# A four-layer fp32 encoder on one core: new head and a 16-block attention pipeline

## The chip, the cores and the metric

The program runs on one core of a Trainium2 chip. The metric is the device time of one execution in microseconds (us), from three runs. The inputs lie in HBM; weights are streamed to SBUF as they are needed.

## The reference

The input is 512 tokens of 1024 features, float32. Two layers alternate: first windowed attention, then latent attention, each followed by a SwiGLU feed-forward network, and an RMS norm ahead of each. Only the first layer's part is touched:

```python
hn = _rmsnorm(h, norm_mix[0])
qkv = hn @ w_qkv                       # 16 query heads, 4 key and 4 value heads of 64
q, k, v = split(qkv)                   # 1024, 256 and 256 columns
q = q * 64 ** -0.5
scores = einsum('q.k') - slope[head] * |pos_q - pos_k|    # per block of 128 queries,
scores = where(|t - s| <= 128, scores, -1e30)             # keys of the block and its neighbours
p = softmax(concat([scores, sink[head]]))[..., :-1]
h = h + (p @ v) @ w_o
```

With 512 tokens there are four query blocks. The two at the ends see 256 keys, the two in the middle 384.

## The kernel before

**Number format.** TensorE reads fp32r. To keep the accuracy of fp32, each operand is split in two: `hi` is the value rounded to fp32r, `lo` is the rest. A product of two tiles is three matmuls into one PSUM bank: hi by lo, lo by hi, hi by hi (`product`, lines 949, 950, 951). So each weight tile (`w_raw`, one of two slots, 128 partitions by 1024 columns) is loaded, rounded to `w_hi` on GpSimd (`w_split_hi`, line 442) and the rest taken on VectorE (`w_split_lo`, line 1473), before TensorE can use it.

**Engines and order.** There is no scheduler: each engine runs a program written out by hand, and the engines are tied by semaphores. TensorE's order sets the order of the work. A wait stalls everything behind it on its engine.

**Head.** The four tiles of x (128 tokens by 1024) land one after the other. TensorE transposes them (line 1021) into the eight banks, one for each 128 features. ScalarE sums the squares of each tile (line 647), then with VectorE copies the transposed x to `h` (lines 654 and 1542). ScalarE makes `x_hi` from `h` (658), VectorE makes `x_lo` (`x_low`, 1548). Then come the projections, three matmuls for each 128 features: two tiles of keys (48 matmuls of 512 columns), the values (96 of 256), and the first two of eight query tiles (48 of 512). Between the values and the queries VectorE scales the keys into `k_dup` (1584, eight instructions) and builds the distance table `near` (1596, 1599). The second query tile's `w_lo` stands behind all of that.

**Attention.** It runs in four groups, one for each key head, with four query heads each. A unit u of a group is one query block n with one head, 16 in a group. Its steps:

- TensorE: scores of 256 or 384 keys, `product` with the keys in `kp_hi`, `kp_lo`. A head fills 64 of the 128 partitions; keys are padded with zeros, so that each of the three matmuls has 128 rows. Three banks are used in turn.
- VectorE: adds the distance and takes the maximum (`read_scores`, 1658), ScalarE: exponential and sum (`expo`, 712), VectorE: reciprocal (1643), GpSimd: scales the row (509).
- TensorE: transposes the four heads' probabilities, 128 keys at a time (1088), ScalarE and VectorE: their hi and lo (718, 1666).
- TensorE: values (`values`, two products for each 128 keys), ScalarE and VectorE: `ot_hi` (722) and `ot_lo` (1671).

At the end of a group the next group's queries (`a_q_out`, 1621; `a_q_lo`, 1627), keys (1606) and values (1613) are made ready. The remaining six query tiles, and in the last group parts of the output projection `w_o`, are put between these steps. The scores of block n+1 come before the transposes of block n, and the values of block n-1 behind them.

**Output projection.** `wo_phase` follows; the profile's TensorE reaches its loop's second tile at 184 us. Everything from there on is not touched.

## Time and profile before

| | us |
|---|---|
| median of 3 runs | 1250.78 (1250.13 to 1253.23) |
| the profiled execution | 1250.18 |
| its span | 1248.4 |
| TensorE busy in the span | 1191.3 (95%) |
| VectorE busy | 630.4 (50%) |
| first product of the head, start | 14.73 |
| first scores, start | 55.48 |
| output projection's loop, start | 184.16 |

The span is the time from the first to the last instruction. TensorE's busy time is modelled: each matmul shows a duration longer than the distance to the next one's start, since they are pipelined. What a matmul costs in a dense stretch is therefore read from the distance between neighbours' starts. The share of busy time is a mean over stages; what the change is worth is read from the stages up to 184 us.

### The profile page before, as it was taken

What the parts mean: (1) busy time and instruction counts of PE and PEld (TensorE: products, weight loads), DVE (VectorE), ACT (ScalarE), POOL (GpSimd) and SP (SyncE); (2) the same over time, 40 slices, a digit from 0 to 9 for tenths busy, and PEclk for the clock granted to TensorE, in tenths of its full rate; (3) what the DMA queues carried; (4) which work ended last, traced back from release to release, by engine and by line L of the source; (5) the groups of instructions that cost most, each with busy time, mean ns of one, the idle gap of its engine ahead of it and who ended that gap; (6) DMA issues with size and microseconds to landing.
All of it is one profiled execution on the core that took longest, in us unless ns stands there. A gap on an engine that the chain in (4) does not pass through costs nothing.

```text
span 1248.4 us, 18246 instructions
## 1 busy us (share of the span) xinstructions
PE 1191.3 (95%) x5796; PEld 992.8 (80%) x5796; DVE 630.4 (50%) x1067; ACT 354.0 (28%) x689; POOL 399.0 (32%) x415
## 2 busy tenths in 40 slices
PE   6899999999999999999889999899999999999996
PEld 5788878788888888888867777678788888888885
DVE  6777764433333433454576776744443333343432
ACT  4266652222200111111365665632222200111101
POOL 3343335333311333343241412325233311323342
PEclk8999999999999999999989999999999999999998
DMA  6211113232433233333200101013333332333421
GB/s 161 68 34 35 35 34 101 85 99 86 119 93 89 87 101 101 109 93 91 70 20 18 36 0 34 18 39 114 97 89 101 103 115 68 101 96 89 120 81 67
DMA packets 176475, 96.67 MB, mean 77 GB/s; under 512 B 8752, under 2 KB 173104, under 8 KB 176432
## 3 DMA queue, kind: packets, MB, share of 16 engines
q1 hardware_dynamic: 176432, 96.12, 26.5%
q8 instruction: 24, 0.39, 0.1%
q14 instruction: 19, 0.16, 0.0%
HBM read 94.01 MB, written 2.10 MB: 77 GB/s over the span
## 4 chain that ended last, share of the span: by engine, by line
PE 80%; DVE 9%; issue 4%; ACT 3%; POOL 2%; DMA 1%; ACTq 0%; DVEq 0%; POOLq 0%; SPq 0%
PE bank L949 26%; PE bank L951 25%; PE bank L950 25%; PE bank L1391 2%; DVE w_lo L1473 1%; POOL w_hi L442 1%; DVE stat L2004 1%; DVE apt_lo L1666 1%; PE bank L1088 1%; DVE s_a L1658 1%; DVE bpt_lo L2009 1%; DMA x_n<-in_x 1%; ACT s_b L880 1%; ACT bpt_hi L886 0%; DVE w_lo L1490 0%
## 5 line engine op out<-in xcount | busy, mean ns | idle before, releaser
L1473 DVE TENSOR_TENSOR w_lo<-w_raw,w_hi 128x1024 fp32r<-128x1024 f32 (+2 forms) x151 | 203.2, 1346 | 297.8 <-POOL w_hi L442 297.7
L442 POOL TENSOR_SCALAR w_hi<-w_raw 128x1024 fp32r<-128x1024 f32 (+3 forms) x159 | 183.3, 1153 | 421.4 <-PE bank L951 410.0
L949 PE MATMUL bank<-x_hi,w_lo 128*128 128x512 f32 x784 | 308.3, 393 | 9.9 <-DVE w_lo L1473 7.7
L951 PE MATMUL bank<-x_hi,w_hi 128*128 128x512 f32 x784 | 306.3, 391 | 0.0
L950 PE MATMUL bank<-x_lo,w_hi 128*128 128x512 f32 x784 | 306.3, 391 | 0.0
L949 PEld LDWEIGHTS bank<-x_hi,w_lo 128*128 128x128 f32 x784 | 147.8, 189 | 42.1 <-DVE w_lo L1473 5.5
L951 PEld LDWEIGHTS bank<-x_hi,w_hi 128*128 128x128 f32 x784 | 147.7, 188 | 30.9
L950 PEld LDWEIGHTS bank<-x_lo,w_hi 128*128 128x128 f32 x784 | 148.0, 189 | 29.7
L949 PE MATMUL bank<-f_hi,w_lo 128*128 128x512 f32 x352 | 137.8, 391 | 1.0 <-DVE f_lo L1776 1.0
L951 PE MATMUL bank<-f_hi,w_hi 128*128 128x512 f32 x352 | 137.1, 389 | 0.0
L950 PE MATMUL bank<-f_lo,w_hi 128*128 128x512 f32 x352 | 137.0, 389 | 0.0
L546 POOL TENSOR_TENSOR gate_s<-gate_s,rs_t 128x512 f32<-128x512 f32 x44 | 56.7, 1290 | 141.7 <-ACT gate_s L769 141.7
L607 POOL TENSOR_SCALAR s_b<-s_b,stat 128x512 f32<-128x512 f32 x64 | 47.3, 741 | 131.5 <-DVE stat L1643 131.3
L1738 DVE TENSOR_TENSOR h<-h,bank 128x512 f32 (+1 forms) x40 | 27.5, 687 | 115.4 <-PE bank L951 115.4
L772 ACT ACTIVATE f_hi<-hid 128x512 f32 x44 | 27.8, 632 | 202.2 <-DVE hid L1774 202.2
L949 PEld LDWEIGHTS bank<-f_hi,w_lo 128*128 128x128 f32 x352 | 66.1, 188 | 15.4 <-DVE f_lo L1776 1.9
L951 PEld LDWEIGHTS bank<-f_hi,w_hi 128*128 128x128 f32 x352 | 66.1, 188 | 13.7
L950 PEld LDWEIGHTS bank<-f_lo,w_hi 128*128 128x128 f32 x352 | 66.1, 188 | 13.5
L769 ACT ACTIVATE gate_s<-gate_t 128x512 f32<-128x512 f32 x44 | 27.8, 632 | 160.5 <-DVE gate_t L1763 160.2
L456 POOL TENSOR_TENSOR ss<-ss,sq 128x512 f32<-128x512 f32 x28 | 52.3, 1870 | 39.6 <-ACT sq L636 39.5
L2009 DVE TENSOR_TENSOR bpt_lo<-bank,bpt_hi 128x512 fp32r<-128x512 f32 x64 | 43.8, 685 | 35.3 <-ACT bpt_hi L886 35.2
L949 PE MATMUL bank<-ot_hi,w_lo 128*128 128x512 f32 x128 | 50.4, 394 | 3.3 <-DVE w_lo L1473 2.6
(219 smaller groups left out, 1863.6 us busy)
## 6 DMA issues: line engine op xcount, KB each, us to landing
w_raw<-in_ffn_w_gu SPq DMA_DIRECT2D x88, 512.0 KB, 3.8
w_raw<-in_ffn_w_down SPq DMA_DIRECT2D x32, 704.0 KB, 4.4
w_raw<-in_a_w_qkv SPq DMA_DIRECT2D x12, 512.0 KB, 3.8
w_raw<-in_a_w_o SPq DMA_DIRECT2D x8, 512.0 KB, 3.6
w_raw<-in_b_w_o SPq DMA_DIRECT2D x8, 512.0 KB, 3.8
w_raw<-in_b_w_in SPq DMA_DIRECT2D x4, 672.0 KB, 4.0
w_raw<-in_b_w_uq SPq DMA_DIRECT2D x4, 576.0 KB, 4.0
x_n<-in_x SPq DMA_DIRECT2D x4, 512.0 KB, 5.3
```

The lines of the kernel that those rows point to most:

```text
L442: pool.tensor_scalar(split_part(w_hi, s, cols, kv), raw_part(s, cols, kv), 1.0, 1.0, ALU.mult, ALU.mult) \
L456: pool.tensor_tensor(n.ss[:], n.ss[:], n.sq[:, b, :], ALU.add).then_inc(ss_ready, 1)
L546: pool.tensor_tensor(gate_s[:], gate_s[:], rs_t[:], ALU.mult).then_inc(silu_rs_ready, 1)
L607: pool.tensor_scalar(view, view, stat[:, 2, u % 8:u % 8 + 1], 1.0, ALU.mult, ALU.mult) \
L769: act.activation(gate_s[:], gate_t[:], ACT.Silu).then_inc(silu_ready, 1)
L772: act.activation(f_hi[:, j, :], hid[:], ACT.Copy).then_inc(f_hi_ready, 1)
L949: pe.matmul(o, ll, rh, start=start, stop=False)
L950: pe.matmul(o, lh, rl, start=False, stop=False)
L951: return pe.matmul(o, lh, rh, start=False, stop=stop)
L1473: dve.tensor_tensor(split_part(w_lo, s, cols, kv), raw_part(s, cols, kv), f(split_part(w_hi, s, cols, kv)), ALU.subtract) \
L1738: dve.tensor_tensor(dst, h[:, m, :], banks[6 + bank_s][:], ALU.add).then_inc(proj_free, 1)
L2009: dve.tensor_tensor(bpt_lo[:, n % 2, i, :], banks[3 + i % 2][:], f(bpt_hi[:, n % 2, i, :]), ALU.subtract).then_inc(pt_free, 1)
```

## The change

It rewrites the program up to the output projection, on all engines.

- **Head.** x_hi and x_lo are made straight from the transposed x in PSUM, and ScalarE alone copies it to `h` afterwards. The key weights are split in halves. The squares of the last x tile are taken later. Eight small matmuls of the identity run ahead of the first product. The features' order is 6, 7, 4, 5, 0, 1, 2, 3. The first two query tiles have buffers of their own (`q_raw0`, `q_raw1`), are loaded right behind the key weights, rounded on ScalarE, and projected right behind the keys; the values come last.
- **Keys.** No zero padding. `ks` holds two key heads in the halves of the 128 partitions, `kx` the same with the halves swapped; four DMAs from SBUF to SBUF write `kx`. All four heads' keys and values are split once, ahead of the attention.
- **Scores.** Each matmul has 64 rows: the upper or the lower half of the array. Those of two heads alternate (partitions 0 to 63, 64 to 127), into two banks.
- **Pipeline.** 16 blocks (a group's query block with its four heads) run in one pipeline over the groups. In slot b TensorE does the scores of block b, the transposes of block b-1 and the values of block b-2, with query or w_o products between them.
- **Weights in the attention.** From the fifth query tile on, `w_hi` is made on ScalarE (`a_w_hi`) and `w_lo` on GpSimd (`a_w_lo`). Reciprocals are taken for two heads at once.

The core of the diff (of the head, the scores and the weights; the slots' order stands in the excerpts below it):

```diff
-            for pos, m in enumerate(K_ORDER):
-                if pos % 2 == 0:
-                    act.wait_ge(pt_done, pos + 2)
-                    act.activation(h[:, K_ORDER[pos + 1], :], banks[K_ORDER[pos + 1]][:], ACT.Copy).then_inc(h_act, 1)
...
-                act.activation(x_hi[:, m, :], h[:, m, :], ACT.Copy, scale=gains[:, 0, m, :]).then_inc(x_hi_ready, 1)
+            def x_high(pos):
+                act.wait_ge(pt_done, pos + 1)
+                act.activation(x_hi[:, K_ORDER[pos], :], banks[K_ORDER[pos]][:], ACT.Copy,
+                               scale=gains[:, 0, K_ORDER[pos], :]).then_inc(x_hi_ready, 1)
...
+            pe.wait_ge(h_act, 1)
+            pe.wait_ge(x_ready, 1)
+            for i in range(8):
+                pe.matmul(banks[6][:, 0:P], ident[:], ident[:], start=True, stop=True)
+            for s in range(2):
+                for pos in range(KD // 2):
+                    k_block(pos, s)
+            for s in range(2):
+                for pos in range(KD // 2, KD):
+                    k_block(pos, s)
+            pe.wait_ge(h_act, 3)
+            spread(norms[0])
...
+            sp.wait_ge(ks_ready, 2)
+            for src, dst in ((ks_hi, kx_hi), (ks_lo, kx_lo)):
+                for half in range(2):
+                    there, here = slice((1 - half) * HD, (2 - half) * HD), slice(half * HD, (half + 1) * HD)
+                    sp.dma_start(f(dst[there, :, :]), f(src[here, :, :])).then_inc(kx_in, 16)
...
-                def scores(u):
-                    n, hd = u // HG, u % HG
-                    k0, nk = A_KB[n]
-                    before = 16 * g + (u - 2 if u >= 3 else (0, -2, -1)[u])
-                    pe.wait_ge(s_free, S_A + before)
-                    q = (slice(None), hd // 2, slice(n * P, (n + 1) * P))
-                    k = (slice(None), hd % 2, slice(k0 * P, (k0 + nk) * P))
-                    product(banks[u % 3][:, 0:nk * P], aq_hi[q], aq_lo[q], kp_hi[k], kp_lo[k], True, True) \
-                        .then_inc(s_done, 1)
+            def a_scores(b, i):
...
+                    pe.wait_ge(a_read, 4 * (b - 1) + 2 * i + 2)
...
+                for k_low, q_low in ((False, True), (True, False), (False, False)):
+                    for odd in range(2):
+                        rows = slice(odd * HD, (odd + 1) * HD)
+                        q = (aq_lo if q_low else aq_hi)[rows, g % 2, i, n * P:(n + 1) * P]
+                        here = odd == g % 2
+                        kt = (ks_lo if here else kx_lo) if k_low else (ks_hi if here else kx_hi)
+                        ins = pe.matmul(banks[A_SCORE_BANKS[2 * i + odd]][:, 0:nk * P], q,
+                                        kt[rows, g // 2, k0 * P:(k0 + nk) * P],
+                                        start=q_low, stop=not (k_low or q_low))
...
+            def a_w_hi(c2, s):
+                act.wait_ge(w_in[s], 16 * c2 + 16)
+                act.wait_ge(w_used, 2 * c2 + s - 1)
+                act.wait_ge(w_hi_ready, 2 * c2 + s)
+                act.activation(w_hi[s][:, 0:W_COLS], w_raw[s][:, 0:W_COLS], ACT.Copy).then_inc(w_hi_ready, 1)
...
+            def a_w_lo(c2, s):
+                pool.wait_ge(w_hi_ready, 2 * c2 + s + 1)
+                pool.wait_ge(w_ready, 2 * c2 + s)
+                pool.tensor_tensor(w_lo[s][:, 0:W_COLS], w_raw[s][:, 0:W_COLS], f(w_hi[s][:, 0:W_COLS]), ALU.subtract)
...
+            for b in range(1, A_BLOCKS + 2):
...
+                elif n == 2:
+                    scores(0)
+                    scores(1)
+                    fill(1)
+                    turn(0)
+                    turn(1)
+                    fill(2)
+                    values(0)
+                    values(1)
+                    turn(2)
```

VectorE's order in the head before, from the first copies of the transposed x (`h` from a bank) on:

```order
L1542 COPY h_49<-bank6 128x512 [waits pt_done]
L1542 COPY h_49<-bank0 128x512 [waits pt_done]
L1548 SCALAR_TENSOR_TENSOR x_lo_51<-h_49,gains_65,x_hi_50 128x512 [waits x_hi_ready,gain_in]
L1473 TENSOR_TENSOR w_lo0_58<-w_raw0_54,w_hi0_56 128x1024 [waits w_hi_ready]
L1548 SCALAR_TENSOR_TENSOR x_lo_51<-h_49,gains_65,x_hi_50 128x512 [waits x_hi_ready]
L1473 TENSOR_TENSOR w_lo1_59<-w_raw1_55,w_hi1_57 128x1024 [waits w_hi_ready]
L1516 TENSOR_SCALAR ms_n_64<-sums_n_72 128x8 [waits x_sq_ready]
L1519 RECIPROCAL rs_n_63<-ms_n_64 128x8 [waits rms_n]
```

The same place now, up to the last key half:

```order
L1740 SCALAR_TENSOR_TENSOR x_lo_51<-bank6,gains_65,x_hi_50 128x512 [waits x_hi_ready,gain_in]
L1747 TENSOR_TENSOR w_lo0_58<-w_raw0_54,w_hi0_56 128x512 [waits k_hi_half]
L1740 SCALAR_TENSOR_TENSOR x_lo_51<-bank7,gains_65,x_hi_50 128x512 [waits x_hi_ready]
L1740 SCALAR_TENSOR_TENSOR x_lo_51<-bank4,gains_65,x_hi_50 128x512 [waits x_hi_ready]
L1740 SCALAR_TENSOR_TENSOR x_lo_51<-bank5,gains_65,x_hi_50 128x512 [waits x_hi_ready]
L1747 TENSOR_TENSOR w_lo1_59<-w_raw1_55,w_hi1_57 128x512 [waits k_hi_half]
L1740 SCALAR_TENSOR_TENSOR x_lo_51<-bank0,gains_65,x_hi_50 128x512 [waits x_hi_ready]
L1747 TENSOR_TENSOR w_lo0_58<-w_raw0_54,w_hi0_56 128x512 [waits k_hi_half]
L1740 SCALAR_TENSOR_TENSOR x_lo_51<-bank1,gains_65,x_hi_50 128x512 [waits x_hi_ready]
L1740 SCALAR_TENSOR_TENSOR x_lo_51<-bank2,gains_65,x_hi_50 128x512 [waits x_hi_ready]
L1747 TENSOR_TENSOR w_lo1_59<-w_raw1_55,w_hi1_57 128x512 [waits k_hi_half]
```

The copies are gone, `x_lo` reads the bank, the key weights' rests come in halves of 512 columns, and the norm's small steps have moved behind them.

TensorE at the start of a group's scores before (group 1; `kp` keys, `aq` queries, all of 128 rows, one head after the other):

```order
L949 MATMUL bank0<-kp_hi_83,aq_lo_81 128x256 [waits s_free,q_ready,kp_ready]
L950 MATMUL bank0<-kp_lo_84,aq_hi_80 128x256
L951 MATMUL bank0<-kp_hi_83,aq_hi_80 128x256
L949 MATMUL bank1<-kp_hi_83,aq_lo_81 128x256 [waits s_free]
L950 MATMUL bank1<-kp_lo_84,aq_hi_80 128x256
L951 MATMUL bank1<-kp_hi_83,aq_hi_80 128x256
L949 MATMUL bank6<-x_hi_50,w_lo0_58 128x512 [waits proj_free,w_ready]
```

And now (group 1, second pair of heads; in this group the even head takes its keys from `kx`, the odd one from `ks`):

```order
L1224 MATMUL bank2<-kx_hi_84,aq_lo_81 128x256 [waits q_ready,a_read]
L1224 MATMUL bank7<-ks_hi_82,aq_lo_81 128x256
L1224 MATMUL bank2<-kx_lo_85,aq_hi_80 128x256
L1224 MATMUL bank7<-ks_lo_83,aq_hi_80 128x256
L1224 MATMUL bank2<-kx_hi_84,aq_hi_80 128x256
L1224 MATMUL bank7<-ks_hi_82,aq_hi_80 128x256
L1083 MATMUL bank6<-x_hi_50,w_lo0_58 128x512
```

There are as many matmuls as before, with the same columns; they alternate between two banks and between the halves of the array.

## Rows read from the trace of the kernel before

**Rows 1.** The page: span, and busy us of each engine.

```profile
span 1248.4 us, 18246 instructions
...
PE 1191.3 (95%) x5796; PEld 992.8 (80%) x5796; DVE 630.4 (50%) x1067; ACT 354.0 (28%) x689; POOL 399.0 (32%) x415
```

**Rows 2.** Windows: busy us of each engine (x instructions), granted clock, DMA.

```profile
14.60:21.40 6.80, 5.91 (x13) 4.26 (x14) 6.42 (x13) 4.24 (x9) 0.78 (x1) 0.50 0.81 143
...
47.20:49.90 2.70, 0.00 (x0) 0.00 (x0) 2.64 (x4) 1.26 (x2) 2.70 (x4) 1.00 0.00 0
...
55.50:182.70 127.20, 122.40 (x785) 108.97 (x783) 93.39 (x280) 76.74 (x203) 43.88 (x78) 1.00 0.12 34
```

**Rows 3.** Waits of TensorE up to 183 us: total us, times, longest.

```profile
PE bank L949 <- DVE w_lo L1473: 7.7, 3, 4.2
```

**Rows 4.** Timeline of TensorE, 4 to 22 us: start, us, instruction, idle before.

```profile
9.44 1.09 PE L1021 MATMUL bank<-ident,x_n 128*128 128x128 f32 x8 [0.41 <-DMA x_n<-in_x]
14.73 0.77 PE L949 MATMUL bank<-x_hi,w_lo 128*128 128x512 f32 x1 [4.20 <-DVE w_lo L1473]
...
18.55 0.63 PE L949 MATMUL bank<-x_hi,w_lo 128*128 128x512 f32 x1
18.98 0.63 PE L950 MATMUL bank<-x_lo,w_hi 128*128 128x512 f32 x1
...
21.71 0.40 PE L951 MATMUL bank<-x_hi,w_hi 128*128 128x512 f32 x1
21.95 0.39 PE L949 MATMUL bank<-x_hi,w_lo 128*128 128x512 f32 x1
```

**Rows 5.** Timeline of TensorE in the attention: starts of neighbours.

```profile
55.59 0.28 PE L950 MATMUL bank<-kp_lo,aq_hi 128*128 128x256 f32 x1
55.71 0.28 PE L951 MATMUL bank<-kp_hi,aq_hi 128*128 128x256 f32 x1
...
59.94 0.34 PE L950 MATMUL bank<-kp_lo,aq_hi 128*128 128x384 f32 x1
60.12 0.33 PE L951 MATMUL bank<-kp_hi,aq_hi 128*128 128x384 f32 x1
...
77.58 0.60 PE L1088 MATMUL bank<-ident,s_a 128*128 128x128 f32 x4
77.93 0.48 PE L949 MATMUL bank<-x_hi,w_lo 128*128 128x512 f32 x1
78.25 0.39 PE L950 MATMUL bank<-x_lo,w_hi 128*128 128x512 f32 x1
```

**Rows 6.** Groups by shape, TensorE, 55.4 to 182.7 us: busy, mean ns, idle.

```profile
L949 PE MATMUL bank<-kp_hi,aq_lo 128*128 128x384 f32 x32 | 11.3, 353 | 0.7 <-DVE stat L1658 0.7
...
L949 PE MATMUL bank<-kp_hi,aq_lo 128*128 128x256 f32 x32 | 10.0, 311 | 0.3
```

**Rows 7.** Groups by shape, VectorE, then ScalarE, 55 to 183 us.

```profile
L1666 DVE TENSOR_TENSOR apt_lo<-bank,apt_hi 128x512 fp32r<-128x512 f32 x40 | 27.3, 685 | 5.8 <-ACT apt_hi L718 5.4
L1658 DVE CUSTOM_DVE_ANT_0 s_a<-near,bank,minus_sink 128x384 f32<-128x384 f32 x32 | 19.2, 599 | 0.9 <-PE bank L951 0.8
...
L712 ACT ACTIVATE s_a<-s_a,stat 128x385 f32<-128x385 f32 x32 | 19.6, 615 | 7.0 <-DVE stat L1658 6.8
```

**Rows 8.** Timeline of VectorE, then GpSimd, in the head.

```profile
11.78 1.56 DVE L1548 SCALAR_TENSOR_TENSOR x_lo<-h,gains,x_hi 128x512 fp32r<-128x512 f32 x1 [0.61 <-ACT x_hi L658]
13.26 1.21 DVE L1473 TENSOR_TENSOR w_lo<-w_raw,w_hi 128x1024 fp32r<-128x1024 f32 x1
...
18.73 1.40 DVE L1548 SCALAR_TENSOR_TENSOR x_lo<-h,gains,x_hi 128x512 fp32r<-128x512 f32 x2
...
11.76 1.04 POOL L442 TENSOR_SCALAR w_hi<-w_raw 128x1024 fp32r<-128x1024 f32 x1 [10.24 <-DMA w_raw<-in_a_w_qkv]
13.84 1.54 POOL L442 TENSOR_SCALAR w_hi<-w_raw 128x1024 fp32r<-128x1024 f32 x1 [1.04 <-DMA w_raw<-in_a_w_qkv]
```

**Rows 9.** The page: a tensor-by-tensor addition on GpSimd.

```profile
L456 POOL TENSOR_TENSOR ss<-ss,sq 128x512 f32<-128x512 f32 x28 | 52.3, 1870 | 39.6 <-ACT sq L636 39.5
```

More of the change, by code:

```diff
@@ L64 @@
 W_UKV = KVL // P * HG * 2 * HD
-U_K, U_Q, U_WOA = 0, 2, 10
+U_K, U_WOA = 0, 2
 U_FFN0 = U_WOA + KD
@@ new lines, in _ @@
+            pe.wait_ge(h_act, 3)
+            spread(norms[0])
+            pe.wait_ge(vec_consts, 1)
+            pe.wait_ge(h_act, 5)
+            for i in range(2):
+                pe.wait_ge(q01_ready, i + 1)
+                for k in range(KD):
+                    at = slice(k * P, (k + 1) * P)
+                    last = product(banks[3 + i][:], q01_hi[i][:, at], q01_lo[i][:, at], x_hi[:, k, :], x_lo[:, k, :],
+                                   k == 0, k == KD - 1)
+                last.then_inc(q01_used, 1)
@@ new lines, in a_v @@
+            def a_v(t):
+                if t == 0:
+                    pe.wait_ge(proj_free, 1)
+                if t == 1:
+                    pe.wait_ge(o_free, O_NORM0 + 1)
+                if t >= 2:
+                    pe.wait_ge(v_ready, t - 1)
+                cols = GROUPS * HD
+                for k in range(KD):
+                    if t == 0 and k % 4 == 0:
+                        pe.wait_ge(w_ready, C_V + k // 4 + 1)
+                    wh, wl = w_block(k // 4, cols, k % 4)
+                    at = slice(t * P, (t + 1) * P)
+                    last = product(banks[6 - t % 2][:, t // 2 * cols:(t // 2 + 1) * cols], x_hi[:, k, at], x_lo[:, k, at],
+                                   wh, wl, k == 0, k == KD - 1)
+                if t < NT - 1:
+                    last.then_inc(v_done, 1)
+                else:
+                    last.then_inc(w_used, 2)
@@ new lines, in a_turn @@
+            def a_turn(b, i):
+                unit = a_unit(b, i)
+                if b == 0 and i < 2:
+                    pe.wait_ge(q_tmp_ready, i + 1)
+                else:
+                    pe.wait_ge(pt_free, unit - 1)
+                for j, hd in enumerate((0, 2, 1, 3)):
+                    if i == 0 and j != 2:
+                        pe.wait_ge(p_ready, 4 * b + hd + 1)
+                    last = pe.transpose(banks[3 + unit % 2][:, j * P:(j + 1) * P],
+                                        s_a[:, b % 2, hd, 1 + i * P:1 + (i + 1) * P], ident[:])
+                last.then_inc(pt_done, 1)
@@ new lines, in a_values @@
+            def a_values(b, i):
+                k0, nk = a_keys(b)
+                pe.wait_ge(pt_free, a_unit(b, i) + 1)
+                if i == 0:
+                    pe.wait_ge(o_free, O_A + b)
+                    if b == 0:
+                        pe.wait_ge(av_zero, 2)
+                        pe.wait_ge(v_ready, NT)
+                for odd in range(2):
+                    at = (2 * (b // NT) + 1 - odd) * HD
+                    v = (slice(None), k0 + i, slice(at, at + P))
+                    p = (slice(None), b % 2, i, slice(2 * P * odd, 2 * P * (odd + 1)))
+                    last = product(banks[5][:, 0:2 * P], av_hi[v], av_lo[v], apt_hi[p], apt_lo[p],
+                                   i == 0 and odd == 0, i == nk - 1 and odd == 1)
+                if i == nk - 1:
+                    last.then_inc(o_done, 1)
@@ new lines, in a_q_step @@
+            def a_q_step(m, k):
+                c = C_Q + m - 2
+                if k == 0:
+                    pe.wait_ge(w_ready, c + 1)
+                    if m == 2:
+                        pe.wait_ge(v_ready, 3)
+                    else:
+                        pe.wait_ge(q_tmp_ready, m)
+                wh, wl = w_block(m % 2, P, k)
+                last = product(banks[6][:], wh, wl, x_hi[:, k, :], x_lo[:, k, :], k == 0, k == KD - 1)
+                if k == KD - 1:
+                    last.then_inc(w_used, 1)
@@ L1547, in x_low, with k_low @@
                 dve.wait_ge(x_hi_ready, pos + 1)
-                dve.scalar_tensor_tensor(x_lo[:, m, :], h[:, m, :], gains[:, 0, m, :], f(x_hi[:, m, :]),
+                dve.scalar_tensor_tensor(x_lo[:, m, :], banks[m][:], gains[:, 0, m, :], f(x_hi[:, m, :]),
                                          ALU.mult, ALU.subtract).then_inc(x_ready, 1)
-            read_x(0)
-            read_x(2)
+            def k_low(s, part):
+                dve.wait_ge(k_hi_half, 2 * s + part + 1)
+                half = K_HALVES[part]
+                dve.tensor_tensor(w_lo[s][:, half], w_raw[s][:, half], f(w_hi[s][:, half]), ALU.subtract) \
+                    .then_inc(w_ready if part else k_lo_half, 1)
```

891 lines of the change are left out of this document (492 added, 399 removed).

## The prediction

> **What bounds the kernel now.** I read the page first: TensorE is busy 95% of the span, and the next engine, VectorE, 50% [rows 1]. So only two things can shorten the run: a stretch where TensorE stands still, and fewer TensorE cycles. The change ends at the output projection, so the second view was TensorE by windows up to 183 us [rows 2], then its waits there [rows 3], then its timeline in the head and the attention [rows 4, 5], then the groups by shape [rows 6, 7] and the other engines in the head [rows 8]. The reader is to see in them: a head in which TensorE first waits and then runs at the lower of its two clock levels (granted clock 0.50, which is 1.2 GHz); a hole of 2.7 us before the second query tile; an attention of 127.2 us that is nearly full of matmuls.
>
> **Prices.** At the full clock neighbours start 0.23 to 0.24 us apart for 512 columns [rows 4], 0.12 for 256 and 0.17 to 0.18 for 384 [rows 5]. I use 0.23, 0.12 and 0.175. Four transposes take 0.35 us (0.09 each), and the matmul behind them holds its successor off for 0.32 instead of 0.23, so leaving the transposes costs 0.09 [rows 5]. At the lower clock 512 columns take 0.43 [rows 4].
>
> **The attention before, as a sum.** 55.5 to 182.7 us is 127.2 us [rows 2]. In it stand 144 query and 48 w_o matmuls of 512 columns (192 x 0.23 = 44.2), 240 of the values (28.8), 192 of the scores, half of each shape [rows 6] (three lines, of which one stands there, with 32 of either shape; 96 x 0.12 + 96 x 0.175 = 28.3), and 160 transposes with 28 exits (14.0 + 2.5). Sum 117.8, so TensorE stands still for about 9.4 us there.
>
> **The change, part by part.**
>
> *Head up to the keys.* Before, the last transposes start at 9.44 and the first product at 14.73, with 4.20 us of waiting for `w_lo` [rows 4]. VectorE's chain in it is x_lo of 1.56 at 11.78, w_lo of 1.21 at 13.26 [rows 8]. Now the copies to h are gone and the first `w_lo` is half as wide (0.6). GpSimd starts its rounding at 11.76, when the weights land [rows 8]; half of its 1.04 puts the first half at 12.3, VectorE adds 0.6 and about 0.4 of hand-over: 13.3. The eight identity matmuls need x_lo and the copy of one bank (about 12.1) and take 8 x 0.11, so they end at 13.0 and are hidden. First product 13.4: gain 1.3. The wait of 0.75 between first and second product (the 7.7 us in three waits are 4.20, 0.75 and 2.72 [rows 3]) goes, since the first tile alone is now used four times: 0.75. The supply: seven more x_lo at 0.70 (1.40 for two) and three half w_lo at 0.6 end at about 20.2 [rows 8]; TensorE needs the last x_lo at 13.4 + 39 x 0.23 = 22.4 at the earliest. So the 48 key matmuls run without a hole.
>
> *The clock.* The granted clock was 0.50 from 14.6 to 21.4 [rows 2], right behind the stretch of 4.2 us in which TensorE had nothing to do. About 16 matmuls started at 0.43 instead of 0.23: 3.2 us. Now the idle stretch is 10.4 to 12.1, and the identity matmuls follow. I take it that the clock stays up: 3.2. Bounds: 3.2 and 0. The Trainium skill, "TensorE: Matmul & The Clock Gate", Part 4, says that transposes don't count as busy for the clock; by that rule the clock would be low at the first product whatever stands between, and the 3.2 us would be lost. The rows speak against it: the page grants 1.00 until 14.6 with nothing but transposes ahead.
>
> *Behind the keys.* The second query tile's hole of 2.72 us [rows 3], a window without one matmul while VectorE is busy 2.64 of 2.70 [rows 2], goes: both query tiles now stand ahead of the values, and the keys' scaling (2 instructions instead of 8), the table and the values' `w_lo` run beside 11.0 us of query matmuls (48 x 0.23). VectorE has some 10 us of work there, so it is just covered; the values might wait up to 1 us. The first query scale needs the query's end, a rounding on ScalarE and a rest on VectorE (three steps of 0.7) before the second pair of block 0's scores: 0.5 us late. New holes in the head: 1.0. Behind the values, query tile 3's weights can be split only when the values' have been used, GpSimd 1.04 and VectorE 1.2, of which scores and transposes of block 1 cover 1.5: 0.8, counted below. The four DMAs to `kx` start when the keys' rests are there (about 30) and have 9 us until the first scores; none of the kind is in the trace, the tiles of 512 KB take 3.8 us from issue to landing. Head in sum: 1.3 + 0.75 + 3.2 + 2.7 - 1.0 = 7.0.
>
> *Scores in halves.* No matmul of 64 rows is in the trace. Bounds for a pair: both at the price of one, 0.12 or 0.175; or one after the other, 0.24 or 0.35. Each still loads its own stationary operand of 128 columns; a transpose shows a load and a matmul every 0.09 [rows 5], so two loads take up to 0.175. I take 0.175 for both shapes: 96 x 0.175 = 16.8, against 28.3: gain 11.5. Bounds 14.2 in all (gain 14.1) and 28.3 (gain 0). The Trainium skill, "TensorEngine Tiling (Array Packing)", Tiling Modes, Key Properties, says that tiles run in parallel but that a change of the mode drains the engine. No row here shows either. There are 38 such changes (19 runs of score matmuls). I price each like the exit from the transposes, 0.09: 3.4 lost. Bounds 0 and 0.16 each (the modelled 0.28 of a matmul less its 0.12 [rows 5]), 6.1.
>
> *The pipeline.* Transposes come a slot behind the scores and values a slot behind them. The four waits of transposes for `apt_lo` and one of the values lay in these 9.4 us. VectorE had 93.4 us of work in 127.2 [rows 2]; six of eight `w_lo`, the padded keys and half of the reciprocals leave it. One slot costs TensorE about 6.6 us, VectorE 4 to 6 (apt_lo 0.69, maximum 0.60 [rows 7]), ScalarE up to 6.3 in the slots with a `w_hi` (four exponentials of 0.62 [rows 7], three roundings of 0.6, one of the weights at 1.0, and two small ones). None is over TensorE, but one is near it. GpSimd's addition of 512 columns takes 1.87 [rows 9], so `a_w_lo` of 1024 takes up to 3.7; behind it stand the next block's scalings, which are needed a slot later, so I cost it at nothing; without that cover it would be 3.7 six times. Of the 9.4 us of stalls I leave 4.5 (0.8 of it the one above, 0.5 at the last values): gain 4.9. Bounds: 2 left, or 12.
>
> Sum: 7.0 + 11.5 - 3.4 + 4.9 = 20.0 us. The profiled execution's 1250.2 gives 1230.2; it lies 0.6 below the median, so the run's median would be 1230.8, and I say 1231.
>
> **Rivals.**
>
> *The halves don't overlap.* The pair takes the time of both: 11.5 less, 1242. For it: each matmul has its own load, and the loads already fill 109 of 127 us [rows 2]. Against it: different rows, different banks, alternating.
>
> *The chain of a block becomes the bound.* Maximum, exponential, reciprocal, scaling, transpose, rounding, rest now all wait for each other over a slot of 6.6 us, where a block took 127.2 / 16 = 7.9. If VectorE's waits for ScalarE (ScalarE at 6.3 in one slot of four, `w_hi` ahead of the exponentials) cost 0.75 a slot, 16 slots give 12: 1243. For it: VectorE is idle for 5.4 us behind ScalarE's `apt_hi` already [rows 7]. Against it: the work between covers most of it.
>
> *The head gives nothing.* Clock low as before and `kx` or the values' weights some us late: 7.0 lost, 1238. For it: SP issues the kx transfers behind everything else.
>
> *Slower.* Each 64-row matmul waits for its load and lets the array run empty: then it costs its modelled duration, 0.31 and 0.35 [rows 6], and 192 of them 63.7 us instead of 16.8: 47 lost, 1278. It decides from 36.8 us of scores on, 0.19 us a matmul. For it: the mode changes. Against it: the order of the loads is the same as now, where they run ahead.
>
> **Chances.** Forecast 0.50; no overlap 0.18; chain 0.14; head 0.08; slower 0.07; that the parts cancel to no change 0.03. The forecast's own range is 1224 to 1237 (overlap at 14.2 and free mode changes below; all mode changes at 0.16 and a low clock above). With the rivals on the fast side, 1222 to 1246 holds 8 in 10. A difference under 0.3% (3.8 us) can't be told from none in this kernel. Faster 0.90, same 0.03, slower 0.07.
>
> **What the profile after would show.** Granted clock 1.00 from the first product on, which starts at 13 to 14 us; keys' matmuls 0.23 apart; scores of block 0 at about 39; block 1 at about 49; pairs of score matmuls that start within a few ns or with 0.175 for two; the output projection's second tile at 164 instead of 184.2. VectorE's waits for ScalarE grow if the chain rules; pairs at 0.24 and 0.35 mean no overlap. The prediction is wrong if the projection starts before 158 or after 176, or if the time behind it changes by more than 3.5 us, the price of one more or one less stretch at the lower clock.

## The result, and the profile after

The changed kernel takes 1235.26 us (median of 4 runs, 1233.6 to 1236.35), the kernel before 1251.18 us beside it. The ratio is 0.987, with a 95% interval of 0.9853 to 0.9887: 16 us faster. Forecast were 1231 us and a range of 1222 to 1246. The profiled execution took 1235.2 us, its span is 1233.1 us.

The page after, span and busy us of each engine (against [rows 1]):

```profile
span 1233.1 us, 18213 instructions
...
PE 1181.3 (96%) x5812; PEld 980.3 (79%) x5812; DVE 609.2 (49%) x1013; ACT 355.8 (29%) x692; POOL 406.4 (33%) x423
```

TensorE is busy 10.0 us less, VectorE 21.2 less, GpSimd 7.4 more. Windows of the changed kernel (busy us and count of each engine, granted clock, DMA), the keys' products and then block 1's scores to the last output projection step that the attention holds (against [rows 2]):

```profile
14.60:21.40 6.80, 6.80 (x31) 5.63 (x31) 5.39 (x9) 6.78 (x11) 0.00 (x0) 1.00 0.79 208
50.10:165.90 115.80, 111.94 (x773) 94.22 (x772) 77.47 (x222) 70.72 (x190) 51.91 (x82) 1.00 0.13 37
```

The keys' products now run at granted clock 1.00 where it was 0.50. The attention is 115.8 us long, without block 0's scores, which stand ahead of it and take 0.9; together 116.7 where it was 127.2. VectorE has 77.5 us of work in it instead of 93.4. Waits of TensorE up to 185 us (total, times, longest; against [rows 3]):

```profile
PE bank L1083 <- DVE w_lo L1669: 2.8, 2, 1.5
PE bank L1164 <- ACT h L736: 1.6, 1, 1.6
PE bank L1240 <- DVE apt_lo L1848: 1.1, 2, 0.9
PE bank L1224 <- DVE aq_lo L1816: 0.7, 1, 0.7
```

The three waits of 7.7 us are gone. In the first line stand a new one of 1.53 us, for query tile 2's weights behind the values, and one of 1.31 at the output projection that both kernels have.

TensorE at the head's turn from transposes to products (start, us, instruction, idle before; against [rows 4]):

```profile
12.08 2.05 PE L1164 MATMUL bank<-ident 128*128 128x128 f32 x16 [1.58 <-ACT h L736]
13.88 0.48 PE L1083 MATMUL bank<-x_hi,w_lo 128*128 128x512 f32 x1
```

The first product starts at 13.88 instead of 14.73. And the first two score pairs of block 2 with their neighbours (against [rows 5]):

```profile
59.39 0.39 PE L1085 MATMUL bank<-x_hi,w_hi 128*128 128x512 f32 x1
59.71 0.44 PE L1224 MATMUL bank<-ks_hi,aq_lo 64*128 64x384 f32 x1
59.71 0.44 PE L1224 MATMUL bank<-kx_hi,aq_lo 64*128 64x384 f32 x1
59.99 0.33 PE L1224 MATMUL bank<-ks_lo,aq_hi 64*128 64x384 f32 x1
...
60.16 0.34 PE L1224 MATMUL bank<-ks_hi,aq_hi 64*128 64x384 f32 x1
...
60.70 0.34 PE L1224 MATMUL bank<-kx_hi,aq_hi 64*128 64x384 f32 x1
60.96 0.50 PE L1083 MATMUL bank<-x_hi,w_lo 128*128 128x512 f32 x1
61.30 0.39 PE L1084 MATMUL bank<-x_lo,w_hi 128*128 128x512 f32 x1
```

Both matmuls of a pair start together (59.71 and 59.71). The next pairs follow 0.175 apart, so a pair costs what one matmul cost in [rows 5]. Around them stand four small losses: 0.32 instead of 0.23 from the last full matmul to the first pair, 0.28 instead of 0.175 behind the first pair, 0.26 instead of 0.175 on leaving, and 0.34 instead of 0.23 behind the first full matmul: 0.4 us a visit. The groups that answer to [rows 7], and the new ones of the weights, 50 to 166 us:

```profile
L1848 DVE TENSOR_TENSOR apt_lo<-bank,apt_hi 128x512 fp32r<-128x512 f32 x40 | 26.9, 685 | 11.4 <-ACT apt_hi L811 11.0
...
L802 ACT ACTIVATE s_a<-s_a,stat 128x385 f32<-128x385 f32 x32 | 19.4, 608 | 5.6 <-DVE stat L1834 5.4
...
L548 POOL TENSOR_TENSOR w_lo<-w_raw,w_hi 128x1024 fp32r<-128x1024 f32 x6 | 14.4, 2406 | 0.0
...
L818 ACT ACTIVATE w_hi<-w_raw 128x1024 fp32r<-128x1024 f32 x6 | 6.3, 1045 | 0.0
```

VectorE waits longer for ScalarE's `apt_hi` than before (11.0 against 5.4) and has time for it. GpSimd's `w_lo` takes 2.4 us, not up to 3.7, and the matmuls that read it don't appear among the waits.

The mark that the prediction calls the output projection's second tile was forecast at 164 and is at 167.39. Where the 16.8 us up to it (from 184.16) come from, against the forecast of 20.0:

| part | forecast | measured |
|---|---|---|
| head, to block 1, without block 0's scores | 7.0 | 6.3 |
| scores' pairs | 11.5 | 14.1 |
| changes of the array's rows | -3.4 | -6.3 to -7.2 |
| stalls in the attention, 9.4 before: gain | 4.9 (4.5 left) | 2.7 to 3.6 (5.8 to 6.7 left) |
| untouched part behind | 0 | -1.5 |

The head is 55.5 less 50.14, plus the 0.9 of block 0's scores. The scores' 14.1 is the count of matmuls at the spacing above. The changes are 18 visits at the 0.35 to 0.40 us that e5 and e2 below give: the prediction counted 19, but the second scores of block 12 and the first of block 13 stand next to each other (135.13 and 135.59 us), which makes one visit of two. The stalls are what 116.7 us leave when the sum of the steps (117.8 less 14.1) and the changes are taken off. Of them 4.5 us can be named: 1.7 for the weights behind the values, and 2.8 in four places of the last group, from 136.7 to 153.9 us, where transposes wait for `apt_lo` and for a scaling and scores for a maximum. Behind the projection's start the span has 1065.7 us instead of 1064.2. Of the total, 16.8 less 1.5 is the 15.3 between the spans.

### The profile page after: what moved, and what is told of

Read it like the earlier page. It is cut to its first block, busy times and chain, and to the rows that moved or that the text cites. A ratio compares the mean times of both kernels' runs of the same rounds, so it can differ in the third digit from the quotient of the medians.

```text
span 1233.1 us, 18213 instructions
## 1 busy us (share of the span) xinstructions
PE 1181.3 (96%) x5812; PEld 980.3 (79%) x5812; DVE 609.2 (49%) x1013; ACT 355.8 (29%) x692; POOL 406.4 (33%) x423
## 4 chain that ended last, share of the span: by engine, by line
PE 84%; DVE 6%; issue 4%; ACT 3%; POOL 2%; DMA 0%; ACTq 0%; DVEq 0%; POOLq 0%
PE bank L1083 26%; PE bank L1085 26%; PE bank L1084 25%; PE bank L1587 2%; PE bank L1240 1%; PE bank L1224 1%; POOL w_hi L482 1%; DVE stat L2215 1%; DVE w_lo L1669 1%; DVE bpt_lo L2220 1%; ACT s_b L1014 1%; PE bank L1158 0%; DVE w_lo L1686 0%; ACT bpt_hi L1020 0%; ACT s_a L802 0%
## 5 line engine op out<-in xcount | busy, mean ns | idle before, releaser
L1669 DVE TENSOR_TENSOR w_lo<-w_raw,w_hi 128x1024 fp32r<-128x1024 f32 (+2 forms) x142 | 191.4, 1349 | 289.1 <-POOL w_hi L482 289.1
L482 POOL TENSOR_SCALAR w_hi<-w_raw 128x1024 fp32r<-128x1024 f32 (+3 forms) x150 | 174.2, 1162 | 404.9 <-PE bank L1085 404.8
L1083 PE MATMUL bank<-x_hi,w_lo 128*128 128x512 f32 x768 | 301.7, 393 | 3.8 <-DVE gate_t L1974 2.2
L1085 PE MATMUL bank<-x_hi,w_hi 128*128 128x512 f32 x768 | 299.1, 389 | 0.0
L1084 PE MATMUL bank<-x_lo,w_hi 128*128 128x512 f32 x768 | 299.0, 389 | 0.0
L1083 PEld LDWEIGHTS bank<-x_hi,w_lo 128*128 128x128 f32 x768 | 144.2, 188 | 35.1 <-DVE gate_t L1974 2.6
L1085 PEld LDWEIGHTS bank<-x_hi,w_hi 128*128 128x128 f32 x768 | 144.2, 188 | 30.5
L1084 PEld LDWEIGHTS bank<-x_lo,w_hi 128*128 128x128 f32 x768 | 144.2, 188 | 29.0
L1084 PEld LDWEIGHTS bank<-f_lo,w_hi 128*128 128x128 f32 x352 | 66.1, 188 | 13.5
L2220 DVE TENSOR_TENSOR bpt_lo<-bank,bpt_hi 128x512 fp32r<-128x512 f32 x64 | 43.8, 686 | 35.3 <-ACT bpt_hi L1020 35.2
L556 POOL TENSOR_SCALAR s_a<-s_a,stat 128x256 f32<-128x256 f32 (+1 forms) x64 | 33.5, 538 | 61.2 <-DVE stat L1843 60.9
```

The source lines that it names most:

```text
L482: pool.tensor_scalar(split_part(w_hi, s, cols, kv), raw_part(s, cols, kv), 1.0, 1.0, ALU.mult, ALU.mult) \
L556: pool.tensor_scalar(view, view, stat[:, 2, u % 8:u % 8 + 1], 1.0, ALU.mult, ALU.mult).then_inc(p_ready, 1)
L1083: pe.matmul(o, ll, rh, start=start, stop=False)
L1084: pe.matmul(o, lh, rl, start=False, stop=False)
L1085: return pe.matmul(o, lh, rh, start=False, stop=stop)
L1669: dve.tensor_tensor(split_part(w_lo, s, cols, kv), raw_part(s, cols, kv), f(split_part(w_hi, s, cols, kv)), ALU.subtract) \
```

## Experiments

For the attention I compare one distance, from block 1's first score to the last values: 111.7 us in the changed kernel (50.14 to 161.83). It is free of what happens in the head and behind. The granted clock is 1.00 all through it in every trace but that of e4.

**Order of a pair.**

```
for k_low, q_low in (...):          ->   for odd in range(2):
    for odd in range(2):                     for k_low, q_low in (...):
```

> The changed kernel, with the six 64-row matmuls of a pair of heads in another order: the three of one head first (rows 0 to 63), then the three of the other (rows 64 to 127), instead of alternating. Nothing else differs. Theory A (two tiles of 64 rows run side by side only when neighbours in the queue lie in different rows): the pairs of one start are gone except where the first head's last meets the second head's first; five steps of 0.12 or 0.175 us instead of three for six matmuls, so 32 x 2 x 0.15 = 9.4 us more than the changed kernel's 1235.3: 1244 to 1246, and the output projection's second tile near 177 instead of 167.4. Rival B (the array keeps separate queues of rows and overlaps whatever stands in the other half): no loss, 1235. Rival C (each 64-row matmul costs its load when the rows repeat): 0.3 us a matmul, 192 x 0.3 = 58 against 14: 1279.

Measured: 1234.52 us, ratio 0.986 (0.9837 to 0.9884), distance 111.7. Rival B holds. TensorE in this kernel, with three matmuls of one head queued ahead of three of the other:

```profile
95.12 0.38 PE L1224 MATMUL bank<-kx_hi,aq_lo 64*128 64x256 f32 x1
95.13 0.38 PE L1224 MATMUL bank<-ks_hi,aq_lo 64*128 64x256 f32 x1
95.34 0.28 PE L1224 MATMUL bank<-kx_lo,aq_hi 64*128 64x256 f32 x1
95.35 0.28 PE L1224 MATMUL bank<-ks_lo,aq_hi 64*128 64x256 f32 x1
```

The other head's `aq_lo` matmul, three places behind in the queue, starts 0.01 us after the first. Alternating is not what gives the overlap.

**Same rows, and all rows.**

```
rows = slice(odd * HD, (odd + 1) * HD)   ->   slice(0, HD)      (e7)
                                         ->   slice(0, P)       (e5)
```

> The changed kernel with the score matmuls of both heads on rows 0 to 63 (the second head then gets the first one's numbers, so its result is not the one wanted; count, columns, banks and order are unchanged). Theory A (the matmuls of e1 overlapped since they lay in different rows, whatever their order): here nothing overlaps, each of 192 takes 0.12 or 0.175 us, 14.1 us more with the visits' cost kept: 1249.5, the first values to the last 14 us longer. Rival B (two 64-row matmuls into different banks overlap whatever their rows): 1235.4. Rival C (in the same rows each waits for its own load to be over): 0.3 us each, 43 us more, 1279.

Measured: 1246.53 us, ratio 0.9952 (0.994 to 0.9965), distance 122.6, 10.9 more. The matmuls follow each other at 0.175 and nothing overlaps:

```profile
93.64 0.33 PE L1224 MATMUL bank<-ks_lo,aq_hi 64*128 64x384 f32 x1
93.81 0.33 PE L1224 MATMUL bank<-kx_hi,aq_hi 64*128 64x384 f32 x1
93.99 0.34 PE L1224 MATMUL bank<-ks_hi,aq_hi 64*128 64x384 f32 x1
```

That is Theory A. The blocks 1 to 15 hold 13.4 of the 14.1 us of doubled steps (7 blocks x 6 x 0.12 and 8 x 6 x 0.175). TensorE's idle steps (starts more than 0.25 us later than the prices of the prediction have them) fall from 4.5 to 1.7 us, as each slot is longer: 13.4 - 2.8 = 10.6, and 10.9 is what came.

> The changed kernel with every score matmul on all 128 rows (the same tiles, both heads' rows at once, so the scores are sums over two heads and not the ones wanted; count, columns and banks are unchanged). It has neither the overlap of two 64-row matmuls nor the change of the array's rows. Theory A (the changed kernel saves 14.1 us by the overlap and pays 19 x 0.4 = 7.6 us for the visits): 6.5 us more, block 1 to the last values 118.2 instead of 111.7 us, 1242.5. Rival B (the prediction's 3.4 us for the changes): 10.7 us more, 1247. Rival C (the 0.4 of a visit is no matter of the rows and stays): 14.1 more, 1250.

Measured: 1240.64 us, ratio 0.9917 (0.9896 to 0.9938), distance 116.9, 5.2 more. On 128 rows a visit has no edges: the first score matmul starts 0.23 behind the last one of 512 columns, and the others follow at 0.12:

```profile
96.66 0.28 PE L1224 MATMUL bank<-kx_hi,aq_lo 128*128 128x256 f32 x1
96.78 0.28 PE L1224 MATMUL bank<-ks_hi,aq_lo 128*128 128x256 f32 x1
96.90 0.28 PE L1224 MATMUL bank<-kx_lo,aq_hi 128*128 128x256 f32 x1
```

Doubled steps 13.4, less 2.1 of idle steps that go, less the price of the 17 visits in this distance, is 5.2: a visit costs 0.36 us. Theory A had 0.4 and was 1.3 too high in sum; the prediction's 0.18 (Rival B) is out by more.

**More visits.**

```
scores(0)                 scores(0)
scores(1)         ->      fill(1)
turn(0)                   scores(1)
fill(2)                   turn(0); fill(1)
```

> The changed kernel, with one step of 128-row matmuls (a query or output projection step of three 512-column matmuls) moved between the first and the second pair of heads in 11 of the 15 blocks 1 to 15, those with block number mod 4 of 1, 2, 3 (block 1 excepted). No matmul is added; only the number of times at which TensorE goes from full rows to 64 rows and back rises, from 19 to 30. Theory A (a visit costs what the trace of the changed kernel suggests, about 0.4 us): 11 x 0.4 = 4.4 us more, 1239.7. Rival B (the prediction's price, 2 x 0.09 a visit): 2.0 us more, 1237.3. Rival C (changes are free and the 0.4 has another reason, such as the wait for a bank): within 0.5 us, 1235.3.

Measured: 1238.75 us, ratio 0.9902 (0.9879 to 0.9924), distance 116.1: 4.4 more for 11 visits, of which 0.5 are idle steps. So 0.35 to 0.40 a visit, with e5's 0.36 between. A visit of three pairs, between a full matmul at either side:

```profile
96.09 0.40 PE L1085 MATMUL bank<-x_hi,w_hi 128*128 128x512 f32 x1
96.42 0.38 PE L1224 MATMUL bank<-kx_hi,aq_lo 64*128 64x256 f32 x1
...
96.64 0.28 PE L1224 MATMUL bank<-kx_lo,aq_hi 64*128 64x256 f32 x1
...
96.77 0.28 PE L1224 MATMUL bank<-ks_hi,aq_hi 64*128 64x256 f32 x1
96.97 0.50 PE L1083 MATMUL bank<-x_hi,w_lo 128*128 128x512 f32 x1
97.31 0.40 PE L1084 MATMUL bank<-x_lo,w_hi 128*128 128x512 f32 x1
```

0.33, 0.22, 0.20 and 0.34 stand where 0.23, 0.12, 0.12 and 0.23 would without edges. Theory A holds.

**The eight identity matmuls.**

```
-            for i in range(8):
-                pe.matmul(banks[6][:, 0:P], ident[:], ident[:], start=True, stop=True)
```

> The changed kernel without the eight matmuls of identity by identity in front of the first product of the keys. Theory A (they hold the clock up after the wait of 1.6 us): a stretch at granted clock 0.50 of some 7 us begins near 14 us, 16 matmuls take 0.43 instead of 0.23 us, 3.2 us more: 1238.5. Rival B (the wait in front of the keys' first product, 10.5 to 13.9 us, is now too short to make the clock fall, and the identity matmuls do nothing): the clock stays at 1.00 and the time is 1235.3, at most 0.3 lower. Where the clock falls in the head it may also fall at another place later, so up to 1.5 us either way can come from the latent attention.

Measured: 1234.18 us, ratio 0.9864 (0.9841 to 0.9887). The first product starts at 12.58 and all behind it at the full clock:

```profile
12.58 0.47 PE L1083 MATMUL bank<-x_hi,w_lo 128*128 128x512 f32 x1 [2.73 <-DVE w_lo L1745]
12.89 0.39 PE L1084 MATMUL bank<-x_lo,w_hi 128*128 128x512 f32 x1
```

By this run Rival B holds, and I took the identity matmuls for useless. e8 and e10 below correct that. The trace shows one of four executions, and a quick one: the weights landed early in it (GpSimd's first rounding starts at 10.63, in e10 at 11.72). Two of the others took 1235.38 and 1236.34 us at a mean granted clock of 0.991 and 0.989, where the profiled one has 0.993; whether the clock fell in their heads isn't known.

**The weights' division put back.**

```
-                        a_w_hi(C_Q // 2 + g + 1, 0)                 (ScalarE)
-                        a_w_lo(C_Q // 2 + g + 1, 0)                 (GpSimd)
+                        w_split_hi(C_Q // 2 + g + 1, 0, W_COLS)     (GpSimd)
+                        w_split_lo(C_Q // 2 + g + 1, 0, W_COLS)     (VectorE)
```

> The changed kernel with the division of the six query and output weights of blocks 2 to 14 put back as in the kernel before: the rounding w_hi on GpSimd (where its subtraction stood), the rest w_lo on VectorE at the end of the same slot; ScalarE has neither. Theory A (the weights were hidden either way; VectorE has 4 to 6 us of work in a slot of 6.6 us): within 1 us of 1235.3. Rival B (VectorE's chain sets the pace of a slot): six times 1.2 us more on VectorE, of which most reaches TensorE, 5 to 7 us: 1241. Rival C (ScalarE was the late one, its rounding of 1.0 us in front of the roundings of the transposes): up to 2 us faster, 1233.5.

Measured: 1245.32 us, ratio 0.9947 (0.9926 to 0.9967), distance 121.2, 9.5 more. None of the three theories was large enough. The waits, 50 to 176 us, then a wait late in the attention and a window behind it:

```profile
DVE w_lo L1666 <- POOL w_hi L482: 8.8, 8, 2.2
...
PE bank L1080 <- DVE ot_lo L1851: 5.7, 4, 2.3
...
147.73 0.35 PE L1080 MATMUL bank<-apt_hi,av_lo 128*128 128x256 f32 x1 [2.34 <-DVE ot_lo L1851]
...
148.88:152.29 3.41, 3.41 (x21) 3.05 (x19) 2.31 (x8) 2.53 (x7) 2.43 (x5) 0.50 0.30 90
```

VectorE now stands still for 8.8 us in front of `w_lo` (e12 below: 1.7), and TensorE waits 5.7 us for `ot_lo`, which VectorE owes it behind that. GpSimd's rounding comes late: it stands behind scalings that wait for VectorE's reciprocals. One part of the 9.5 us is the clock: behind the wait of 2.34 us it stood at 0.50 from 148.88 to 152.29 us, and set against the changed kernel, matmul by matmul, TensorE fell back there from 7.7 to 9.2 us, by 1.6.

> Half of e4: ScalarE keeps the rounding w_hi at the head of the slot, as in the changed kernel, and only the rest w_lo is taken back to VectorE, where e4 had it (behind the last reciprocal of block 4g, behind the last apt_lo of block 4g+2); GpSimd has neither. From block 1's scores to the last values the changed kernel takes 111.7 us and e4 121.2. Theory A (VectorE, with 1.2 us more in six slots, is what made e4 slow): 119 to 121 us, and the time is near 1243. Rival B (e4's loss came from GpSimd's rounding, which stood behind scalings that wait for the reciprocals and so came too late, and VectorE stood still behind it): 112 to 113.5 us, the time near 1236.

Measured: 1239.85 us, ratio 0.9905 (0.9875 to 0.9935), distance 114.9, 3.2 more. Neither theory alone: of e4's 9.5 us 3.2 are VectorE's added work and 1.6 the fallen clock; the other 4.7 came with the rounding that was late on GpSimd and held VectorE up. This holds for the places I chose in the slots; other places were not tried.

**Query tile 2's weights in halves.**

```
 pool: w_hi[0] in two halves;  dve: w_lo[0] half by half
 dve:  w_lo[1] behind a_pt_lo(0, 1) of block 1, instead of ahead of its maxima
 pe:   a_q_step(2, 0) waits for the first half, a_q_step(2, 4) for the second
```

> The changed kernel with the split of query tile 2's weights done in two halves (GpSimd rounds columns 0 to 511, VectorE takes their rest while GpSimd does the others), and query tile 3's rest on VectorE moved behind the work of block 1. Theory A (TensorE's wait of 1.53 us at 53.6 us is the whole chain of one rounding of 1.0 and one rest of 1.6 us, and only the first half is needed): the wait falls to 0.1 to 0.4, 1.2 us less up to the output projection (second tile's start 166.2 instead of 167.4). Rival B (the first transposes of block 1 or its maximum are next and take the gain): under 0.4 us. In the time either may be masked by up to 1.5 us in the latent attention, according to where the clock falls there: 1232.5 to 1235.5.

Measured: 1233.59 us, ratio 0.986 (0.9839 to 0.9881), distance 111.2, 0.5 less. The two places on TensorE:

```profile
52.42 0.50 PE L1088 MATMUL bank<-x_hi,w_lo 128*128 128x512 f32 x1
...
60.81 0.47 PE L1088 MATMUL bank<-x_hi,w_lo 128*128 128x512 f32 x1 [0.91 <-DVE q_tmp L1819]
```

The wait at the first product of query tile 2 is gone, but the first product of tile 3 now waits 0.91 us for the scaling of tile 2, since the moved `w_lo` stands ahead of it on VectorE. Rival B, though with another name in it than I had.

**Combinations.**

```
e8:  e6; no identity matmuls; a_v(0), a_v(1), scores of block 0, a_v(2), a_v(3)
e9:  e6; the same order of the values; w_lo[1] between block 1's two reciprocals;
     the output projection's third tile with its weights in halves too
e10: e9 without the identity matmuls
```

> The halved weights, the identity matmuls left out, and block 0's scores behind the second tile of the values instead of the first (with that tile's two steps on ScalarE and VectorE in front of block 0's exponentials and maxima), so that the second query tile's rest is ready in time. Theory A (each takes away a wait that ended last): 1.2 for the weights, 1.3 for the identity matmuls, 0.7 to 1.3 for the query's rest: the output projection 3.2 to 3.8 us earlier than in the changed kernel, and with the cold stretch in the latent attention at its cheap place another 1.5: 1230.5 to 1232. Rival B (block 0's later chain makes block 1's transposes wait): 1 to 2 us of it lost, 1233.

Measured: 1234.44 us, ratio 0.9867 (0.9846 to 0.9889). No faster than e6, and slower than either theory had it. In its head TensorE waited 3.0 us for `w_lo`, and eight matmuls behind it started 0.43 us apart, 1.6 us in all. Neither theory had that.

> The changed kernel with the identity matmuls kept and four waits attacked: query tile 2's weights in halves; tile 3's rest moved on VectorE between block 1's two reciprocals; block 0's scores behind the second tile of the values; the third output projection tile's weights in halves too. Theory A (the waits of 1.53, 0.69 and 1.31 us go or shrink to 0.4 and nothing takes their place): the output projection's third tile starts 2.5 to 3.2 us earlier than 167.4, at 164.2 to 164.9, and the time is 1232 with the costly place of the cold stretch in the latent attention, 1230.5 with the cheap one. Rival B (as in e6, a third to a half of it comes back as a wait for the next thing VectorE owes): 1.2 us, 1234.

Measured: 1231.3 us (5 runs, 1230.49 to 1232.91), ratio 0.984 (0.9823 to 0.9856), the fastest kernel of the study. The changed kernel, run again beside it (e11), took 1233.03 us: 1.7 more by the medians, 3.3 by the ratios (0.0026 x 1251), with intervals that overlap. So the times alone don't settle the gain; the trace does, for the part that was changed. At the mark of 167.39 it shows

```profile
164.78 0.50 PE L1096 MATMUL bank<-ot_hi,w_lo 128*128 128x512 f32 x1 [0.61 <-DVE w_lo L1998]
```

2.6 us earlier, though its first product came 0.48 us later (14.36): 3.1 us gained in between, as Theory A had it. The wait is 0.61 instead of 1.31.

> The kernel e9 without the eight identity matmuls. Theory A (they matter in the executions in which the weights land late: with a wait of 2.7 us in e3 the clock stayed up, with one of 3.0 in e8 eight matmuls behind it started at 0.43 us): where the wait in front of the first product is 2.7 or less, the time equals e9's or is up to 0.5 lower; where it is 3.0 or more, the granted clock falls behind it for 3.5 us and it costs 1.5 to 2 us. Rival B (e8's cold stretch had nothing to do with them): a cold stretch in the head shows up in e9 as often as here.

Measured: 1233.01 us, ratio 0.985 (0.9825 to 0.9875). The window behind the first product without the identity matmuls:

```profile
14.60:18.00 3.40, 3.40 (x10) 2.58 (x9) 3.40 (x7) 3.40 (x6) 0.13 (x1) 0.52 0.77 180
```

and with them (e9):

```profile
14.60:18.00 3.40, 3.40 (x16) 2.78 (x16) 3.40 (x7) 3.40 (x6) 0.06 (x1) 1.00 0.68 158
```

TensorE without them, at the first product and where the clock has fallen:

```profile
13.67 0.47 PE L1096 MATMUL bank<-x_hi,w_lo 128*128 128x512 f32 x1 [2.90 <-DVE w_lo L1777]
...
15.02 0.63 PE L1098 MATMUL bank<-x_hi,w_hi 128*128 128x512 f32 x1
15.44 0.63 PE L1096 MATMUL bank<-x_hi,w_lo 128*128 128x512 f32 x1
```

The wait was 2.90 us here and the clock fell 1 us behind it, 3.0 us in e8 with the same, 2.73 us in e3 and it stayed up. All ten traces with the identity matmuls show 1.00 in this stretch. The length of the wait doesn't decide alone: in e4's attention the clock fell 1.15 us behind a wait of only 2.34 us, with TensorE busy 5.55 of the 8.88 us before. The identity matmuls hold the first product back (in the changed kernel the half `w_lo` ends at 12.3 and the product starts at 13.88, in e3 it starts at 12.58, of which 0.7 us are left at block 1: 49.46 against 50.14), and are worth some 1.5 (eight starts at 0.43 instead of 0.23) in the executions in which the weights land late. At the mark e10 is 0.9 us behind e9 (165.70 and 164.78). Three traces without them are few; what made the clock stay up in e3 and fall in e8 and e10 stays open.

**The changed kernel again.**

> The changed kernel itself once more, for the untouched part behind it. From the start of the latent projections to the first values of the latent attention the traces show 42.2 to 42.6 us in before, e2, e3, e4, e5, e6 and 43.8 in the changed kernel, e1 and e7; the granted clock falls 21 to 23 us behind the start in the ones and 26.5 in the others. Theory A (which of the two comes is a matter of the execution, not of the kernel): this trace may show either, and over executions the time scatters by 1.5 us; seeing 42.3 here settles it. Rival B (the change or what lies where in memory fixes it): 43.8 again.

Measured: 1233.03 us (1232.72 to 1237.12), ratio 0.9866 (0.9842 to 0.9889). From the first transposes of the latents to the first values of the latent attention, in the changed kernel's first trace:

```profile
593.98 0.38 PE L1472 MATMUL bank<-ident,lat 128*128 128x128 f32 x2
...
637.76 0.48 PE L1083 MATMUL bank<-bpt_hi,bv_lo 128*128 128x512 f32 x1
```

and in its second one:

```profile
593.70 0.38 PE L1472 MATMUL bank<-ident,lat 128*128 128x128 f32 x2
...
635.88 0.48 PE L1083 MATMUL bank<-bpt_hi,bv_lo 128*128 128x512 f32 x1
```

43.8 and 42.2 us, with the same instructions. The windows at the lower clock, of the first and of the second:

```profile
620.40:627.50 7.10, 6.91 (x25) 6.01 (x25) 3.36 (x9) 4.08 (x13) 4.11 (x6) 0.52 0.01 3
```

```profile
615.37:622.20 6.83, 6.71 (x17) 4.74 (x16) 5.17 (x12) 3.88 (x9) 2.07 (x3) 0.50 0.00 1
```

In the first the clock falls 26.4 us behind those transposes and TensorE then has 25 matmuls to do at half speed; in the second it falls 21.7 us behind them, at 615.37, and there are 17. Over all traces: with one stretch that begins 20 to 23 us behind the transposes, 42.2 to 42.6 us (before, e2, e3, e4, e5, e6, e11); beginning at 26.4 to 26.7 (the changed kernel, e10), or with a second one behind it (e1, e7, e9), 43.8 to 43.9 (e12, with a second one too, 43.1); with a stretch of only some 3 us (e8), 41.2. Theory A holds: the 1.5 us lost behind the change is a matter of the execution. The times show it too: of the nine executions of the kernel before that ran beside e11, the five at a mean granted clock of 0.989 to 0.991 took 1249.0 to 1250.9 us, the four at 0.987 1252.4 to 1252.9.

## Why the prediction was right, point by point

*Head up to the keys, 1.3 and 0.75.* First product at 13.88 where I had 13.4, so 0.85 instead of 1.3. VectorE was earlier than I had it, at about 12.3, since the weights landed earlier in this execution (GpSimd starts at 10.58 instead of 11.76; in e1, e4, e7 and e9 it starts near 11.7 and `w_lo` ends at 13.4 to 13.5, as I had it). But the identity matmuls, which I took for hidden by 13.0, last until the product: they start at 12.08, and the record counts 16 of them, twice as many as are written, so they take 1.8 us where I had 0.9. The wait between first and second product is gone as forecast, and the 48 matmuls run without a hole.

*Clock, 3.2.* Right in size. The reason is half mine: I named the shorter idle stretch and the identity matmuls together. e3, e8 and e10 take the identity matmuls away: with the shorter wait alone the clock stayed up once (2.73 us) and fell twice (2.90 and 3.0). The Trainium skill, "TensorE: Matmul & The Clock Gate", Part 4, has PE's transpose mode not count as busy; e3 speaks against it once more, with nothing but transposes ahead of a first product at 12.58 and 1.00 behind it. In e8 and e10 too the clock is at 1.00 at the first product, and falls about 1 us later.

*Behind the keys.* The 2.72 us hole is gone. Of the 1.0 us of new holes 0.69 came, at the second pair of block 0 (`aq_lo`), plus that visit's edges. Block 0 at 39.47 (forecast 39), block 1 at 50.14 (49). The wait for the weights behind the values is 1.53 us, not 0.8. TensorE waited for the first of two `w_lo`, which ended at 53.52:

```profile
51.46 2.05 DVE L1669 TENSOR_TENSOR w_lo<-w_raw,w_hi 128x1024 fp32r<-128x1024 f32 x1 [0.23 <-POOL w_hi L482]
...
53.44 1.21 DVE L1669 TENSOR_TENSOR w_lo<-w_raw,w_hi 128x1024 fp32r<-128x1024 f32 x1
```

I had 1.2 for it, which is what the second took. The first ran beside GpSimd's rounding of the other weights (51.40 to 52.45) and took 2.05. That the rounding is the cause isn't shown by a run of its own. What the wait was worth is shown by e6: only 0.5.

*Scores in halves, 11.5.* The overlap is whole, 14.1 us, the end of the bounds. I had taken 0.175 for a pair of 256 columns, for two loads that follow each other; the pairs behind the first stand 0.12 apart (0.13 in e2's lines), and the loads of a pair start together too (59.70 and 59.71 us in block 2), so the loads overlap as the matmuls do. The rival of no overlap is out; the slower one too.

*Mode changes, 3.4.* This is the step that was mis-sized. I priced a change like an exit from transposes, once, 0.09. Each change costs twice, at the first matmul and at the one behind it, about 0.2 us, 0.35 to 0.40 for in and out (e2, e5, the timeline). The 18 visits cost 6.3 to 7.2 us, above my upper bound of 6.1. The Trainium skill, "TensorEngine Tiling (Array Packing)", Key Properties, has that a change drains the engine: the trace agrees, with 0.2 us a change.

*The pipeline, 4.9.* Stalls left 5.8 to 6.7 instead of 4.5. I gave all of the gain to the order of the slots and treated `w_hi` on ScalarE and `w_lo` on GpSimd as a danger, at no gain. e4 shows the reverse: without that division the attention is 9.5 us longer, 7.9 without the fallen clock, more than the pipeline's whole gain, so in the places tried the gain rests on it. The rival of the chain did not come in this kernel. e4 comes near it in size, but there VectorE waited for GpSimd's rounding, not for ScalarE.

*Untouched part, 0.* 1.5 us longer in the profiled execution, within the 3.5 allowed, and e11 shows it gone. With it, the second execution's span is 1230.8.

So the sum of 20.0 came out as 16.8 in the profiled executions: 2.6 better on the overlap, 2.9 to 3.8 worse on the changes, 1.3 to 2.2 worse on stalls, 0.7 in the head; and 1.5 behind it that belongs to the execution. The direction and the main terms held; two errors of opposite sign hid each other.

## What to carry to other kernels

Where a contraction has only 64 rows, put the two heads in different halves of the array: the second matmul is free, in both orders tried. Then keep such matmuls together, since going in and out costs 0.35 to 0.40 us a visit; three pairs at 256 columns save 0.36 and no more than pay for it, six pairs at 384 save 1.05. When a pipeline's slot is nearly as long as an engine's work, look at where an operation stands behind one that waits, before its duration: the rounding that came late cost 4.7 us and the clock that fell behind one of its waits 1.6, the work itself 3.2. And compare a stage by marks on both sides of it, and look at the granted clock inside it, since the stretches at the lower clock moved by themselves and were worth 1.5 us.
